# Hybrid decoder layer on one core: the norm row spread into PSUM by a product, z gated once per head, and the late weight and u sums of z's Winograd scheme on VectorE

## Chip, core and metric

The kernel runs on one core of a Trainium2 chip. The metric is device time in microseconds (us) from start to end of the program; the kernel before was run three times on the device: 1046.83, 1048.23 and 1048.41 us, median 1048.23. One more execution was taken with a profile, and all rows below are from that one.

## What is computed

One decoder layer over 16 learned meta tokens and 1024 tokens of width 1024, in fp32:

```python
u = rmsnorm(h, norm_w)                       # h: 1040 x 1024
proj = u @ w_in                              # 1024 x 7184, split into
q, k, v, g_attn, c_b, c_c, c_h, g_conv, z, xbc, dt = split(proj)
y_attn = diff_attention(q, k, v) * silu(g_attn)      # 4 heads
y_conv = short_conv(c_b, c_c, c_h) * silu(g_conv)
y_ssm  = group_norm(ssd_scan(xbc, dt) * silu(z))     # 16 heads in 4 groups
h = h + concat(y_attn, y_conv, y_ssm) @ w_out
out = rmsnorm(h, final_norm_w)[16:]
```

## The kernel before, in words

All products run on TensorE as three fp32r products of high and low parts (high x high, high x low, low x high). A matrix is split by a copy into fp32r (high) and a subtraction (low).

Every engine runs its own queue in the order of hand-written lists of steps: `ahead()` and `BETWEEN` (the x stage), `Z_ACT`, `Z_DVE` and `z_run` of each engine (the z stage), `BEHIND` (its name in the program is `PRE`: the first q, k, v pieces and the dt row), then `schedule()`, once for each of four heads (attention, short convolution, state scan), and at last the output product. Semaphores hold a step until what it reads is there.

**The x stage** (`ahead`, lines 195 to 222). Nine tiles of x (tile 0 is the 16 meta tokens) are loaded, squared and summed on ScalarE (`x_square`), raised to -1/2 on GpSimd (`x_power`, L1047 `power`), scaled on VectorE by that factor and the norm row (`x_scale`, L1462), turned on TensorE (`x_turn`, L1870) into PSUM banks 2 and 3, and split into `u_hi` (`x_high`, ScalarE, L1251) and `u_lo` (`x_low`, VectorE, L1468). The norm row is loaded by a DMA that repeats it over 128 partitions of `lot` (`norm_load`, L890). For tiles 5 to 8, `s1` (L1473) keeps the sum of the two halves of u.

**z** (1024 tokens x 1024 columns) is made by Winograd's scheme: seven products of half the size, in this order: M_11, M_12, M_S2, M_S1, M_S3, M_S4, M_22. Each has four slots (a slot is a quarter of the inner dimension: 4 token tiles x 3 matmuls of 512 columns, L1904). The slots of M_11 and M_12 (0 to 7) are `z_early`, woven between the turns of the x stage, three tile-slots per x tile; slots 8 to 27 are `z_run` on TensorE. Weights come in four blocks T1 to T4 of 1 MB (`z_weights`, each as two DMAs of 512 KB); `z_sum` makes T1-T3, T2-T1, T2-T3 and T4-T2 in place on GpSimd (L1072), after which T2 is loaded a second time for M_S4. The sums of u are `s2` (from `s1`; tiles 0 and 1 on GpSimd, L1077, 2 and 3 on VectorE, L1478) and `s3` (8 steps of two instructions, GpSimd, L1089 and L1090). Weight slots are split by `z_high` (ScalarE, L1196) and `z_low` (L1064 on GpSimd up to slot 7, L1497 on VectorE from slot 8). `z_acc` (ScalarE, L1224) copies a bank out of PSUM, `z_add` (VectorE, L1504) adds a second one to it. Each finished 128 x 512 block is gated here: `z_tanh` (ScalarE, L1235), `z_gate` (VectorE, L1508), 16 of each; then it is stored (`z_store`) to a DRAM scratch, from which each head loads its 128 x 8 x 256 slice (`z_load`, at the end of its attention).

**The state scan of a head** (`schedule`, from `add("chunk", 0)`, line 343). `chunk` c turns and scales the inputs of chunk c (TensorE, then VectorE L1732 to L1739) and multiplies the decay matrix by C.B (L1743, what TensorE's `scan` c needs); `decay` c makes that matrix (ScalarE, L1349 and L1352) from a row that a DMA brings. The end of `scan` on VectorE multiplies by z (L1762). Between the steps, `fill` puts projection pieces (L1885, 3 matmuls for each of 8 slices of the inner dimension) on TensorE. The order on VectorE is chunk 0, chunk 1, scan 0, chunk 2, scan 1, and so on; on ScalarE, decay 1, decay 2.

Of the kernel before, what the change touches and what calls it, by code (L numbers as in the profile page):

```python
# [194 lines left out]
def ahead():  # L195

    out = [("x_load", 0), ("x_load", 1), ("norm_load", 0), ("x_load", 2), ("z_weights", ("T3", 0)), ("x_load", 3),
# [4 lines left out]
    for r in range(-3, CH):  # L202
# [34 lines left out]
def schedule(last):  # L237
# [114 lines left out]
    for c in range(1, CH + 3):  # L352
# [52 lines left out]
Z_ACT = [*[("z_acc", (0, t)) for t in range(4)], ("s2_high", 0), ("s2_high", 1), ("z_high", 8), ("z_high", 9), ("s2_high", 2), ("s2_high", 3), ("z_tanh", (0, 0)), ("z_tanh", (0, 1)),  # L405
         ("z_high", 10), ("z_high", 11), ("z_tanh", (0, 2)), ("z_tanh", (0, 3)), *[("s1_high", t) for t in range(4)], ("z_high", 12),
# [44 lines left out]
def build(nc, x, meta_tokens, norm_w, w_in, w_out, attn_lambda, attn_norm_w, sconv_w, ssm_conv_w,  # L451
# [6 lines left out]
    with ExitStack() as ctx:  # L458
# [105 lines left out]
        norm_row = lot[:, 0:D]  # L564
# [12 lines left out]
        z_th = [lot[:, HALF * n:HALF * (n + 1)] for n in range(2)]  # L577
        s_f = z_th
# [89 lines left out]
        u_ps = [ps[:, 2, :], ps[:, 3, :]]  # L668

# [168 lines left out]
        def _(eng):  # L838
# [187 lines left out]
        def _(eng):  # L1026
# [22 lines left out]
            def z_run():  # L1049
                iteration(-1, [("s2", 0, 1), ("s2", 1, 1), ("z_sum", ("T2", 1), 1), ("z_sum", ("T3", 0), 1), ("z_sum", ("T3", 1), 1),  # L1050
                               *[("s3", (M_S3, k), 1) for k in range(ZK)], ("z_sum", ("T4", 0), 1), ("z_sum", ("T4", 1), 1),
                               *[("s3", (M_S4, k), 1) for k in range(ZK)]])

            def iteration(i, steps):
                for step, a, d in steps:
# [9 lines left out]
                    elif step == "z_sum":  # L1065
                        name, half = a
                        x, y, done = {"T1": ("T1", "T3", 0), "T2": ("T2", "T1", 1 + half), "T3": ("T2", "T3", 3 + half), "T4": ("T4", "T2", 3 + half)}[name]
                        if name in ("T1", "T2"):
                            eng.wait_ge(z_in[name], 32)
# [3 lines left out]
                    elif step == "s2" and a < 2:  # L1073
# [4 lines left out]
                        eng.tensor_tensor(to, to, u_lo[:, 0:ZK, cols].bitcast(F32), ALU.subtract).then_inc(s2p_ok, 1)  # L1078
                    elif step == "s3":

                        p, k = a
                        cols = slice(META + HALF, L) if p == M_S3 else slice(META, META + HALF)
                        q = (M_S3, M_S4).index(p) * ZK + k
                        if q == 0:
                            eng.wait_ge(z_out_ok, 4)
# [1101 lines left out]
```

## Time and profile before

| | |
|---|---|
| runs | 1046.83, 1048.23, 1048.41 us |
| profiled execution | 1048.38 us |
| its span, first to last instruction | 1046.7 us |
| TensorE busy | 1002.3 us (96%) |
| VectorE, ScalarE, GpSimd busy | 693.0, 465.1, 315.1 us |
| x and z stage | from 0 to 119.75 us |
| heads, and the output product | the rest |

Times in rows are microseconds from the start of the span; PE is TensorE, DVE VectorE, ACT ScalarE, POOL GpSimd, SP the queue that issues the DMAs. L1904 is line 1904 of the kernel. A row of a timeline gives start and duration; in brackets stands how long the engine was idle before it, and what ended that.

### The profile page before, as it was taken

The page shows a single profiled execution, that of the slowest core. Times are in us where ns is not written, and L with a number is a line of the kernel's source. Part 1 is how long each engine was busy: PE and PEld are TensorE (multiplying, and loading weights), DVE is VectorE, ACT ScalarE, POOL GpSimd, SP SyncE. Part 2 cuts the span into 40 slices and gives each one's busy share as a digit, 9 for nine tenths or more (in the row PEclk, how much of TensorE's full clock was granted, in tenths as well). Part 3 has the DMA queues.
Part 4 walks back from the last instruction along what each step waited for, and adds up shares of the span by engine and source line. Part 5 has one row for each costly group of instructions (what it writes and reads, how often), then busy time and mean ns, then how long its engine had stood idle before and what let it go on. Part 6 is the DMA issues. An engine that isn't in the chain of part 4 may idle for free.

```text
span 1046.7 us, 15633 instructions
## 1 busy us (share of the span) xinstructions
PE 1002.3 (96%) x5745; PEld 895.0 (86%) x5745; DVE 693.0 (66%) x1238; ACT 465.1 (44%) x1057; POOL 315.1 (30%) x250
## 2 busy tenths in 40 slices
PE   5879999999999999999999999999999979999997
PEld 4657879998989999899899988989998877888885
DVE  5899553777566268656526865663686757698866
ACT  6554333342445443344634433454343454534555
POOL 5956210333333233323321423332151431000002
PEclk9999999999999999999999999999999999999999
DMA  8013402033412303332140333122233330994323
GB/s 343 1 41 103 144 21 84 25 118 101 120 52 71 121 21 121 101 111 61 54 133 26 121 101 111 54 59 92 71 121 100 92 111 2 361 394 146 94 59 161
DMA packets 106807, 110.61 MB, mean 106 GB/s; under 512 B 6374, under 2 KB 76108, under 8 KB 106732
## 3 DMA queue, kind: packets, MB, share of 16 engines
q1 hardware_dynamic: 106732, 109.62, 32.2%
q8 instruction: 46, 0.75, 0.3%
q14 instruction: 29, 0.24, 0.1%
HBM read 84.36 MB, written 25.24 MB: 105 GB/s over the span
## 4 chain that ended last, share of the span: by engine, by line
PE 81%; DVE 6%; issue 5%; POOL 4%; ACT 2%; DMA 1%; SPq 0%; DVEq 0%; ACTq 0%; POOLq 0%
PE ps L1885 45%; PE ps L1894 15%; PE ps L1870 4%; PE ps L2096 3%; PE ps L1904 2%; PE ps L2130 2%; PE ps L2074 2%; PE ps L2075 2%; POOL w_lo L1059 1%; PE ps L2132 1%; PE ps L2136 1%; DVE work L1462 1%; DMA acum_b<-in_w_in 1%; POOL lot L1090 1%; POOL lot L1089 1%
## 5 line engine op out<-in xcount | busy, mean ns | idle before, releaser
L1885 PE MATMUL ps<-u_hi,w_hi 128*128 128x348 f32 (+3 forms) x1024 | 365.2, 357 | 1.8 <-POOL w_lo L1059 1.8
L1885 PE MATMUL ps<-u_lo,w_hi 128*128 128x348 f32 (+3 forms) x1024 | 347.8, 340 | 0.0
L1885 PE MATMUL ps<-u_hi,w_lo 128*128 128x348 f32 (+3 forms) x1024 | 347.2, 339 | 0.0
L1885 PEld LDWEIGHTS ps<-u_hi,w_hi 128*128 128x128 f32 x1024 | 193.5, 189 | 15.0 <-POOL w_lo L1059 2.1
L1059 POOL TENSOR_TENSOR w_lo<-w_raw,w_hi 128x1024 fp32r<-128x1024 f32 x48 | 117.5, 2450 | 293.3 <-ACT w_hi L1183 293.3
L1885 PEld LDWEIGHTS ps<-u_hi,w_lo 128*128 128x128 f32 x1024 | 192.9, 188 | 11.0
L1885 PEld LDWEIGHTS ps<-u_lo,w_hi 128*128 128x128 f32 x1024 | 193.3, 189 | 10.4
L1047 POOL TENSOR_TENSOR small<-small,m_half 128x1 f32<-128x1 f32 (+2 forms) x57 | 46.0, 809 | 311.4 <-DVE small L1824 143.9
L1667 DVE TENSOR_REDUCE small<-ps 128x1 f32<-128x144 f32 (+7 forms) x64 | 49.6, 774 | 82.2 <-PE ps L2078 81.6
L1331 ACT ACTIVATE work<-ps,small 128x144 f32<-128x144 f32 (+7 forms) x64 | 48.1, 751 | 53.8 <-DVE small L1667 53.8
L1870 PE MATMUL ps<-ident,work 128*128 128x128 f32 (+2 forms) x393 | 59.2, 281 | 8.0 <-DVE u_lo L1468 4.4
L1359 ACT ACTIVATE y_n<-y_n,small 128x256 f32<-128x256 f32 x32 | 16.3, 509 | 111.4 <-POOL small L1047 111.4
L1743 DVE TENSOR_TENSOR lm_buf<-lm_buf,lot 128x512 f32<-128x512 f32 x32 | 25.1, 784 | 58.2 <-PE ps L2136 41.6
L1894 PE MATMUL ps<-q_hl 128*128 128x512 f32 x264 | 62.1, 389 | 0.0
L1870 PEld LDWEIGHTS ps<-ident,work 128*128 128x128 f32 (+2 forms) x393 | 45.9, 139 | 14.9 <-issue 9.4
L1894 PEld LDWEIGHTS ps<-q_hl 128*128 128x128 f32 x264 | 49.5, 188 | 10.3
L1349 ACT ACTIVATE lm_buf<-acum_b,sg 128x128 f32<-128x128 f32 x128 | 40.8, 389 | 22.2 <-DMA acum_b<-acum_scratch 16.1
L1183 ACT CAST w_hi<-w_raw 128x1024 fp32r<-128x1024 f32 x48 | 49.8, 1040 | 0.1
L2096 PE MATMUL ps<-conv_b_s,conv_g 128*128 128x128 f32 x288 | 39.3, 282 | 0.0
L1104 POOL TENSOR_TENSOR xdd<-xdt,sg 128x256 f32<-128x256 f32 (+1 forms) x32 | 20.5, 645 | 62.3 <-DVE xdt L1732 62.3
L2074 PE MATMUL ps<-k_hl,q_hl 128*128 128x512 f32 (+4 forms) x112 | 37.8, 338 | 0.3
L2075 PE MATMUL ps<-k_hl,q_hl 128*128 128x512 f32 (+4 forms) x112 | 36.3, 335 | 0.0
(391 smaller groups left out, 1855.3 us busy)
## 6 DMA issues: line engine op xcount, KB each, us to landing
w_raw<-in_w_in SPq DMA_DIRECT2D x48, 512.0 KB, 4.4
acum_b<-acum_scratch SPq DMA_DIRECT2D x32, 256.0 KB, 4.4
acum_b<-in_w_out SPq DMA_DIRECT2D x22, 256.0 KB, 4.6
work<-in_x SPq DMA_DIRECT2D x8, 512.0 KB, 9.4
work<-in_w_out SPq DMA_DIRECT2D x16, 256.0 KB, 4.1
t_scratch<-work SPq DMA_DIRECT2D x16, 256.0 KB, 2.3
t_scratch<-acum_b SPq DMA_DIRECT2D x16, 256.0 KB, 2.6
work<-z_scratch SPq DMA_DIRECT2D x4, 1024.0 KB, 5.3
```

The costliest lines, as they stand in the source:

```text
L1047: return eng.tensor_tensor(to[0:rows_, n:n + w], of[0:rows_, n:n + w], m_half[0:rows_, 0:w], ALU.pow)
L1059: eng.tensor_tensor(w_lo[:, a % 2, :, :], w_raw[:, a % 2, :, :], w_hi[:, a % 2, :, :].bitcast(F32), ALU.subtract).then_inc(w_lo_ok, 1)
L1183: eng.copy(w_hi[:, b, :, :], w_raw[:, b, :, :]).then_inc(w_hi_ok, 1)
L1331: eng.activation(prob[m][:, 0:nk], s_ps[:, 0:nk], ACT.Exp, bias=mx[:, m:m + 1], accum_out=psum_e[:, s % 2, m:m + 1]).then_inc(exp_ok, 1)
L1349: ins = eng.activation(lmat[:, a % 2, r, :], acum_b[:, a % 2, r, :], ACT.Relu, bias=sg[:, 1, a, r:r + 1], scale=-1.0)
L1667: eng.tensor_reduce(mx[:, m:m + 1], s_ps[:, 0:nk], AX.X, ALU.max, negate=True).then_inc(max_ok, 1)
L1870: return eng.transpose(dst, src, ident[0:n, 0:n])
L1885: ins = eng.matmul(dst, w[:, k, 0:m], u[:, k, cols], start=(k == 0 and n == 0), stop=(k == KD - 1 and n == 2))
L1894: ins = eng.matmul(ps[:, BANKS[n // KS][t], :], y[:, at], w, start=(begins and m == 0), stop=(ends and m == 2), skip_group_check=True)
L2074: eng.matmul(s_ps[:, at:end], q_hi[m][:, qs], k_st[m][:, at:end], start=True, stop=False)
L2075: ins = eng.matmul(s_ps[:, at:end], q_lo[m][:, qs], k_st[m][:, at:end], start=False, stop=not masked)
L2096: eng.matmul(o_ps[:, P:2 * P], a_t[:, n, :], v_blk[:, n, :], start=(n == 0), stop=False)
```

## The change

- The norm row is loaded once (4 KB, first in SP's queue) and spread over 128 partitions by two fp32 products with a row of ones into PSUM banks 5 and 6 (`norm_row`); `x_scale` reads it there. M_12's first two tiles, which use these banks, now wait for the last `x_scale`.
- In the x stage GpSimd does the sums for T1 two rounds earlier (rounds 2 and 3), T2's first in round 5, T2's second in round 7, and all four `s2`.
- `s3` and the sums for T3 and T4 move from GpSimd's `z_run` into `Z_DVE`, each two or three steps ahead of its use.
- z is stored without the gate (z's third block by `z_acc` (2, t) instead of tanh and gate out of PSUM). Each head gates its slice in two halves of 128 x 1024: `z_tanh` 0 and `z_gate` 0 after `decay` 1 and in front of chunk 1; `z_tanh` 1 and `z_gate` 1 behind chunk 2. They use `th_tile`.
- `w_dt`'s DMA counts on the semaphore of the other parameter rows.

```diff
 def ahead():
-    out = [("x_load", 0), ("x_load", 1), ("norm_load", 0), ("x_load", 2), ("z_weights", ("T3", 0)), ("x_load", 3),
+    out = [("norm_load", 0), ("norm_row", 0), ("x_load", 0), ("x_load", 1), ("x_load", 2), ("z_weights", ("T3", 0)), ("x_load", 3),
...
         if r >= 5:
             out.append(("s1", r - 5))
+            if r == 7:
+                out.append(("z_sum", ("T2", 1)))
+            if r >= 6:
+                out.append(("s2", r - 6))
...
 BETWEEN = [...
-           ("z_high", 4, 2), ("z_low", 4, 2), ("z_high", 5, 3), ("z_low", 5, 3), ("z_high", 6, 4), ("z_low", 6, 4), ("z_high", 7, 5), ("z_low", 7, 5),
-           ("z_sum", ("T1", 0), 5), ("z_sum", ("T1", 1), 6), ("z_sum", ("T2", 0), 7)]
+           ("z_high", 4, 2), ("z_low", 4, 2), ("z_sum", ("T1", 0), 2), ("z_sum", ("T1", 1), 3), ("z_high", 5, 4), ("z_high", 6, 4), ("z_low", 5, 4), ("z_low", 6, 4),
+           ("z_high", 7, 5), ("z_low", 7, 5), ("z_sum", ("T2", 0), 5)]
...
     add("chunk", 0)
     add("decay", 1)
+    add("z_tanh", 0)
+    add("z_gate", 0)
...
         if c < CH:
             add("chunk", c)
+        if c == 2:
+            add("z_tanh", 1)
+            add("z_gate", 1)
...
+Z_ACT = [("s2_high", 0), ("s2_high", 1), ("z_high", 8), ("s2_high", 2), ("z_acc", (0, 0)), ("z_acc", (0, 1)), ("s2_high", 3), ("z_acc", (0, 2)), ("z_acc", (0, 3)),
+         *[("z_high", n) for n in (9, 10, 11)], *[("s1_high", t) for t in range(4)], ("z_high", 12),
...
-         *[("z_tanh", (1, t)) for t in range(4)], *[("z_high", n) for n in range(23, 28)], *[("z_tanh", (2, t)) for t in range(4)]]
+         *[("z_high", n) for n in range(23, 28)], *[("z_acc", (2, t)) for t in range(4)]]
...
+Z_DVE = [("s2_low", 0), ("s2_low", 1), ("z_low", 8), ("s2_low", 2), ("s2_low", 3), ("z_low", 9), ("z_low", 10), ("z_low", 11), *[("z_add", (0, t)) for t in range(4)],
+         *[("s1_low", t) for t in range(4)], ("z_low", 12), ("s3", (M_S3, 0)), ("s3", (M_S3, 1)), ("z_low", 13), ("s3_low", (M_S3, 0)), ("s3", (M_S3, 2)), ("z_sum", ("T3", 0)),
+         ("z_low", 14), ("s3_low", (M_S3, 1)), ("s3", (M_S3, 3)), ("z_sum", ("T3", 1)), ("z_low", 15), ("z_low", 16), ("s3_low", (M_S3, 2)), ("s3", (M_S4, 0)),
+         ("z_low", 17), ("s3_low", (M_S3, 3)), ("s3", (M_S4, 1)), ("z_low", 18), ("s3_low", (M_S4, 0)), ("s3", (M_S4, 2)), ("z_sum", ("T4", 0)),
+         ("z_low", 19), ("s3_low", (M_S4, 1)), ("s3", (M_S4, 3)), ("z_sum", ("T4", 1)), ("s3_low", (M_S4, 2)), ("z_low", 20), ("s3_low", (M_S4, 3)), ("z_low", 21),
+         ("z_low", 22), *[("z_add", (1, t)) for t in range(4)], *[("z_low", n) for n in range(23, 28)]]
...
-        norm_row = lot[:, 0:D]
+        norm_row = lot[0:1, 0:D]
...
-        z_th = [lot[:, HALF * n:HALF * (n + 1)] for n in range(2)]
+        z_th = th_tile[:, 0:D].rearrange("p (c n) -> p c n", c=QB // 2)
...
+        norm_ps = ps[:, 5:7, :].rearrange("p b n -> p (b n)")
...
-                        eng.dma_start(norm_row, norm_w[0, :].partition_broadcast(P)).then_inc(norm_in, 16)
+                        eng.dma_start(norm_row, norm_w[0:1, :]).then_inc(norm_in, 16)
...
             def z_run():
-                iteration(-1, [("s2", 0, 1), ("s2", 1, 1), ("z_sum", ("T2", 1), 1), ("z_sum", ("T3", 0), 1), ("z_sum", ("T3", 1), 1),
-                               *[("s3", (M_S3, k), 1) for k in range(ZK)], ("z_sum", ("T4", 0), 1), ("z_sum", ("T4", 1), 1),
-                               *[("s3", (M_S4, k), 1) for k in range(ZK)]])
+                iteration(-1, [("s2", 3, 1)])
...
                     elif step == "z_tanh":
...
+                        eng.wait_ge(z_n_in, 16 * (it + 2))
+                        if a == 0:
+                            eng.wait_ge(conv_ok, it * 4 + 5)
                         else:
...
+                            eng.wait_ge(z_out_ok, it * 2 + 1)
+                        eng.activation(z_th, z_n[:, 4 * a:4 * a + 4, :], ACT.Tanh, scale=0.5).then_inc(z_th_ok, 1)
...
                     elif step == "z_gate":
...
+                        half = slice(4 * a, 4 * a + 4)
+                        eng.wait_ge(z_th_ok, it * 2 + a + 1)
+                        eng.scalar_tensor_tensor(z_n[:, half, :], z_th, 1.0, z_n[:, half, :], ALU.add, ALU.mult).then_inc(z_out_ok, 1)
...
-                            eng.wait_ge(z_n_in, 16 * (it + 2))
+                            eng.wait_ge(z_out_ok, it * 2 + (a - 1) // 4 + 1)
...
+                    elif step == "norm_row":
+                        eng.wait_ge(norm_in, 16)
+                        for h in range(2):
+                            ins = eng.matmul(norm_ps[:, HALF * h:HALF * (h + 1)], ones[0:1, :], norm_row[:, HALF * h:HALF * (h + 1)], start=True, stop=True)
+                        ins.then_inc(norm_pe, 1)
...
+                            if ZY_BANKS[t] in (5, 6) and p == M_12:
+                                eng.wait_ge(x_n, CH)
```

SP's wait for `z_sum_ok` 8 (all eight sums) in front of T2's second load stands in both versions.

## Rows read from the trace of the kernel before

**Rows 1.** Waits of TensorE, whole span: total, times, longest.
```profile
PE ps L1904 <- DVE w_lo L1497: 9.2, 5, 3.9
```

**Rows 2.** Timeline of PE: restarts in the x and z stage, and the first projection.
```profile
39.76 0.89 PE L1870 MATMUL ps<-ident,work 128*128 128x128 f32 x4 [1.84 <-DVE xd L1473]
...
56.05 0.50 PE L1904 MATMUL ps<-w_hi,k_hl 128*128 128x512 f32 x1 [3.89 <-DVE w_lo L1497]
...
97.66 0.50 PE L1904 MATMUL ps<-w_hi,q_hl 128*128 128x512 f32 x1 [0.34 <-DVE w_lo L1497]
...
119.75 0.32 PE L1885 MATMUL ps<-u_hi,w_hi 128*128 128x348 f32 x1
```

**Rows 3.** Windows: busy us (instructions) of PE, PEld, DVE, ACT, POOL; PEclk, DMA share, GB/s.
```profile
10.00:20.00 10.00, 6.15 (x23) 5.24 (x24) 6.52 (x12) 6.66 (x13) 7.20 (x7) 1.00 1.04 415
...
56.00:60.00 4.00, 3.95 (x11) 3.18 (x12) 4.00 (x7) 2.23 (x5) 0.00 (x0) 0.63 0.04 8
```

**Rows 4.** Timeline of POOL: a z_low, the last power, a sum alone, an s3 beside DVE.
```profile
29.68 1.27 POOL L1064 TENSOR_TENSOR q_hl<-lm_buf,q_hl 128x512 fp32r<-128x512 f32 x1
...
33.85 0.55 POOL L1047 TENSOR_TENSOR small<-small,m_half 128x1 f32<-128x1 f32 x1
34.37 2.37 POOL L1072 TENSOR_TENSOR conv_b_s<-conv_b_s,acum_b 128x1024 f32<-128x1024 f32 x1
...
66.88 1.74 POOL L1089 TENSOR_TENSOR lot<-u_hi,w_raw 128x512 f32<-128x512 f32 x1
```

**Rows 5.** DMA issues: size, us from issue to landing; and SP's issue of T1's second half.
```profile
lot<-in_norm_w SPq DMA_DIRECT2D x1, 512.0 KB, 5.3
...
conv_b_s<-in_w_in SPq DMA_DIRECT2D x1, 512.0 KB, 13.3
...
th_tile<-in_w_in SPq DMA_DIRECT2D x1, 512.0 KB, 4.9
...
10.33 0.49 SPq L897 DMA_DIRECT2D conv_b_s<-in_w_in  x1
```

**Rows 6.** Timeline of DVE: x_scale 8, x_low 7, one s2 instruction, four z_add, a 128x1024 two-operand product.
```profile
34.54 3.28 DVE L1462 SCALAR_TENSOR_TENSOR work<-work,small,lot 128x1024 f32<-128x1024 f32 x1
37.74 1.28 DVE L1468 TENSOR_TENSOR u_lo<-ps,u_hi 128x512 fp32r<-128x512 f32 x2
...
53.98 0.68 DVE L1478 TENSOR_TENSOR w_raw<-y_n,u_hi 128x512 f32<-128x512 f32 x1
...
99.55 2.48 DVE L1504 TENSOR_TENSOR ys<-ps,ys 128x512 f32<-128x512 f32 x4
...
881.20 1.22 DVE L1718 TENSOR_TENSOR conv_y<-conv_y,conv_b_s 128x1024 f32<-128x1024 f32 x1
```

**Rows 7.** Timeline of ACT: last instruction of decay 1 in the first, third and last head.
```profile
267.80 0.63 ACT L1352 ACTIVATE lm_buf<-lm_buf 128x512 f32<-128x512 f32 x1
...
641.07 0.64 ACT L1352 ACTIVATE lm_buf<-lm_buf 128x512 f32<-128x512 f32 x1
...
826.71 0.63 ACT L1352 ACTIVATE lm_buf<-lm_buf 128x512 f32<-128x512 f32 x1
```

**Rows 8.** Chain of waits, pieces in order of time (start, us): scan 1 on PE, same heads.
```profile
271.99 0.84 PE ps L2130 x8
...
644.39 0.84 PE ps L2130 x8
...
828.70 0.84 PE ps L2130 x8
```

**Rows 9.** Timelines of ACT and DVE, first head: a tanh, a gating product, chunk 1's first and last steps.
```profile
260.77 1.08 ACT L1316 ACTIVATE th_tile<-work 128x1040 f32<-128x1040 f32 x1 [2.93 <-DVE work L1645]
...
261.88 1.24 DVE L1654 SCALAR_TENSOR_TENSOR work<-th_tile,work 128x1040 f32<-128x1040 f32 x1 [0.48 <-ACT th_tile L1316]
...
264.26 0.42 DVE L1732 TENSOR_TENSOR xdt<-ps,sg 128x256 f32<-128x256 f32 x1
...
268.46 0.69 DVE L1743 TENSOR_TENSOR lm_buf<-lm_buf,lot 128x512 f32<-128x512 f32 x1 [2.93 <-ACT lm_buf L1352]
```

More of the change, by code:

```diff
@@ L576, in build @@
         s2_f = w_raw_flat.rearrange("p (k n) -> p k n", k=ZK)
-        z_th = [lot[:, HALF * n:HALF * (n + 1)] for n in range(2)]
-        s_f = z_th
+        z_th = th_tile[:, 0:D].rearrange("p (c n) -> p c n", c=QB // 2)
+        s_f = [lot[:, HALF * n:HALF * (n + 1)] for n in range(2)]
         z_tmp = [[work[:, D * 4 + HALF * t:D * 4 + HALF * (t + 1)] for t in range(4)],
@@ L1072, in iteration @@
                         eng.tensor_tensor(z_w[name][half], z_w[x][half], z_w[y][half], ALU.subtract).then_inc(z_sum_ok, 1)
-                    elif step == "s2" and a < 2:
+                    elif step == "s2":
                         cols = slice(META + P * a, META + P * (a + 1))
@@ L1077, in iteration @@
                         own(eng, eng.tensor_tensor(to, s1_f[a].rearrange("p (k n) -> p k n", k=ZK), u_hi[:, 0:ZK, cols].bitcast(F32), ALU.subtract))
[L1078 to L1085, printed above, removed]
[L1086 to L1090 removed]
+                        eng.tensor_tensor(to, to, u_lo[:, 0:ZK, cols].bitcast(F32), ALU.subtract).then_inc(s2_ok, 1)
                     elif step == "x_power":
@@ L1473, in iteration @@
                         eng.tensor_tensor(s1_f[a], u_ps[1], s1_f[a], ALU.add).then_inc(s1_ok, 1)
-                    elif step == "s2" and a >= 2:
-                        cols = slice(META + P * a, META + P * (a + 1))
-                        to = s2_f[:, :, P * a:P * (a + 1)]
-                        eng.wait_ge(s1_ok, a + 1)
-                        own(eng, eng.tensor_tensor(to, s1_f[a].rearrange("p (k n) -> p k n", k=ZK), u_hi[:, 0:ZK, cols].bitcast(F32), ALU.subtract))
-                        eng.tensor_tensor(to, to, u_lo[:, 0:ZK, cols].bitcast(F32), ALU.subtract).then_inc(s2d_ok, 1)
+                    elif step == "s3":
+                        p, k = a
+                        cols = slice(META + HALF, L) if p == M_S3 else slice(META, META + HALF)
+                        q = (M_S3, M_S4).index(p) * ZK + k
+                        if q == 0:
+                            eng.wait_ge(norm_pe, 1)
+                            eng.wait_ge(s2_ok, 4)
+                        if q >= 2:
+                            eng.wait_ge(s_lo_ok[M_S3 if q - 2 < ZK else M_S4], (q - 2) % ZK + 1)
+                        own(eng, eng.tensor_tensor(s_f[q % 2], u_hi[:, ZK + k, cols].bitcast(F32), s2_f[:, k, :], ALU.subtract))
+                        eng.tensor_tensor(s_f[q % 2], s_f[q % 2], u_lo[:, ZK + k, cols].bitcast(F32), ALU.add).then_inc(s3_ok, 1)
+                    elif step == "z_sum" and a[0] in ("T3", "T4"):
+                        name, half = a
+                        x, y = {"T3": ("T2", "T3"), "T4": ("T4", "T2")}[name]
+                        eng.wait_ge(z_sum_ok, 3 + half)
+                        eng.tensor_tensor(z_w[name][half], z_w[x][half], z_w[y][half], ALU.subtract).then_inc(z_sum_ok, 1)
                     elif step == "s2_low":
```

69 lines of the change are left out of this document (23 added, 46 removed).

## Prediction, made before the result

> **What bounds the kernel now.** I read the page's busy shares first: TensorE works 96% of the span, so a change can win only in a stretch where it waits. The view of its waits places most of them: 9.2 us for `z_low` on VectorE (L1497) [rows 1], all in the z stage. The timeline of TensorE shows where: idle 1.84 us before tile 8's turn at 39.76, 3.89 us before M_S2 at 56.05, a short wait before M_S4 at 97.66; M_22 ends and the projections begin at 119.75 [rows 2]. From 97.66 on it runs through: 96 matmuls in 22.09 us, 0.230 us each. After the long wait the granted clock averaged 0.63 from 56 to 60 [rows 3], so a wait can cost more than its length. Everything behind 119.75 is a row of projections: what ends the z stage earlier moves all of it, and a wait added in a head adds to it. So there are two sums, the front's and the heads'.
>
> **The front: x stage.** GpSimd now does T1's first sum in round 2, and that sum waits for T1's weights. Today the second half is issued at 10.33 and lands 13.3 us later, at 23.6 [rows 5]. The 512 KB norm load ahead of it [rows 5] shrinks to 4 KB; at 415 GB/s [rows 3] that is 1.3 us, so 22.3. From there GpSimd's queue is the clock of the x stage, since `x_power` of tiles 5 to 8 stands behind the sums: to the end of power 8, three sums of 2.37, three `z_low` of 1.27 and four powers of 0.55 [rows 4], 13.1 us, make 35.4, against 34.4 now (33.85 + 0.55) [rows 4]. A later power, but `x_scale` 8 took 3.28 us with both operands in SBUF while GpSimd summed; the `x_low` pair behind it reads one operand from PSUM and took 1.28 for two, also beside a GpSimd sum [rows 6]. I take 1.3 for `x_scale` from PSUM (bounds 1.3 and 3.3), as that is the nearer kind. It ends at 36.8 instead of 37.8; two `x_low` and an `s1`, 1.9 us, then tile 8's turn at 38.8 instead of 39.76. The two M_12 tile-slots that now wait for `x_scale` 8 fit before it. Behind it TensorE has 14 tile-slots x 3 x 0.230 and two sets of turns of about 0.4: 10.4 us, M_12's end at 49.2, against 52.2 now (56.05 - 3.89) [rows 2].
>
> Norm product: no row shows it; between nothing and several us. It delays the first `x_scale`s, which run ahead of T1's landing, and that cover I count as holding: nothing. If it is gone, tiles 5 to 8 slip by as much. The norm load now stands first in SP's queue, so each x load issues about 0.5 us later [rows 5]; same cover.
>
> **The front: z stage.** After power 8, GpSimd does `s2` 0, T2's second sum, and `s2` 1 to 3: eight instructions of 1.27 and one of 2.37, 12.5 us, to 47.9, if nothing disturbs it; 1.74 each where VectorE interleaves two-operand steps [rows 4], up to 1.9 for four of them: 49.8. I take 49.5, because `Z_DVE` begins at about 42.5. The Trainium skill, SBUF — State Buffer, section "Who interferes with whom", has the shared port pair as an exclusive lock held for the whole instruction, the loser blocked; by that rule four whole VectorE steps of 0.62 would stand in GpSimd's way, `s2` 3 would end about 0.6 us later and so would the sum. Behind `s2` 3, ScalarE has `s2_high` 3, two `z_acc` and `z_high` 9, about 2.3 us: VectorE takes `z_low` 9 at 51.8.
>
> From there VectorE has no wait in my walk, and no competitor, as GpSimd's queue is empty: to T4's second sum it has 25 single steps of 0.62 (four took 2.48), eight `s3` of two instructions of 0.68, four sums of 1.22 [rows 6]: 15.5 + 10.9 + 4.9 = 31.3 us, so 83.1. Then SP, which waits for all eight sums, reloads T2: the second issue about 0.5 us behind, 4.9 to landing [rows 5]: 88.5; `z_high` 20 and `z_low` 20, 1.2 us: M_S4 starts at 89.7 instead of 97.66. TensorE itself could be there sooner: M_S2 from 49.2, with M_S1 and M_S3 48 matmuls each, 33.1 us, and about 3 us waiting for `z_acc` (3, 0), which ScalarE reaches only behind `s3_high`: 85.3. So **T2's reload is late next**, and it covers whatever the clock costs before. M_S4 and M_22 are the same 22.1 us; the projections begin at 111.8, 8.0 us earlier. The wait before M_S4 is some 4 us; one of 3.89 us was followed by four at 0.63 [rows 2, 3], 1.5 us lost. I take half: the **front gains 7.2**, bounds 4 and 9.
>
> The weight splits of the first pieces need M_S4's last bank, `z_acc` (2, t), two casts and two GpSimd subtractions: some 9 us beside M_22's 11. The removed 16 tanh and 16 gates lay on ScalarE and VectorE beside products; M_S4's path is in the walk, the others were covered. `w_dt`'s shared semaphore: nothing, as SP issues that load and the rows in one go, in front of the first projection weights. SP's stores wait for less than before.
>
> **The heads.** `z_gate` 0 stands on VectorE between chunk 0 and chunk 1, and waits for `z_tanh` 0, which ScalarE reaches only after decay 1. Queued behind it is all of chunk 1, with L1743, for which TensorE's scan 1 waits. In the first head decay 1 ends at 268.43 [rows 7] and scan 1 starts at 271.99 [rows 8]: 3.56 us. Now to go between: tanh 1.08, gate 1.24, chunk 1's small steps 1.27 (264.26 to 265.53, that is 268.46 - 2.93), L1743 0.69 [rows 9], together 4.28. TensorE waits 0.7. The second head repeats it (0.7 taken). In the third decay ends at 641.71 and scan 1 starts at 644.39: 2.68, so 1.6. In the last, which has half the fill between the scans, 827.34 and 828.70: 1.36, so 2.9 [rows 7, 8]. The sum is 5.9; bounds 4 (if the decay row lands sooner) and 8 (if the lower clock follows the long wait in the last head). The second half's tanh and gate (2.3 us) fall in VectorE's wait for scan 1 on TensorE: 0.1. **The heads lose 6.0.** Projections follow without slack, so these add up.
>
> **Sum.** The profiled execution took 1048.38, 1.7 over its span, and 0.15 over the median. 1048.4 - 7.2 + 6.0 = **1047.2**, 1.0 under the median. A measurement can tell about 0.2% (2.1 us) from no change.
>
> **Rivals.**
> - *The gate hides.* If decay 1 starts about 1.5 us sooner in every head, or TensorE arrives later, the heads cost about 1, and the front's gain stands: 1042. For it: decay waits for a DMA, and its end varies by 0.9 us against scan 1 between the first and third head [rows 7, 8]. Against: no edit moves that DMA. Chance 0.2.
> - *The VectorE list is slower than its steps.* One mechanism: `Z_DVE` now holds `s3` and the sums, and every step that has to wait for ScalarE pushes T4's last sum and so T2's reload. If M_S4 starts after 93.6 (front gain under 4.1), the heads outweigh it by over 2.1 us; at 95.5 the gain is 2.2 and the time 1052. For it: three engines pass `s3`, high and low round; against: in the walk ScalarE is ready each time. Chance 0.2.
> - *PSUM doesn't free `x_scale`* (the change doesn't do that part): 2.0 us more on `x_scale` 8, 1049; part of the forecast's range.
>
> **How the numbers follow.** Forecast 0.6, centred on 1047.2, 1044.5 to 1049.5 by itself; a third of it lies under 1046.1 (0.2% faster), the rest within 0.2%. With the rivals: faster 0.2 + 0.2 = 0.4; same 0.4; slower 0.2. The range for 8 in 10 takes in the first rival's centre and stops just short of the second's: 1042 to 1051.5.
>
> **What would show it.** Right: POOL's T1 sum in the low twenties with power 5 behind it; `x_scale` at 1.3; T4's last sum near 83 on DVE, T2's issue behind it, M_S4 near 90; the first L1885 near 112; and in each head a TensorE wait at L2130 for L1743, longest in the last. Wrong: no such wait in the heads, or M_S4 starting at the end of M_S3 without one, or after 93.6.

## The result, and the profile after

The change made the kernel slower: 1051.81 us, the median of 8 runs, against 1048.37 for 8 runs of the kernel before on the same chip, ratio 1.0023, 95% interval 1.0012 to 1.0033. Forecast was 1047.2, range 1042 to 1051.5. The profiled execution took 1051.7, its span 1049.9, 3.2 more than before.

First the waits of TensorE in the changed kernel (total, times, longest):

```profile
PE ps L1876 <- ACT y_n L1354: 7.4, 6, 4.0
PE ps L2143 <- DVE lm_buf L1749: 5.1, 4, 2.7
PE ps L1910 <- DVE w_lo L1503: 4.0, 1, 4.0
PE ps L1891 <- POOL w_lo L1069: 1.8, 1, 1.8
```

The first line stands for `y_n`, a chunk's output after gate and norm, which TensorE turns at the end of its scan; it was 7.0 in six before. The 9.2 us for `z_low` [rows 1] have become one wait of 4.0, and the waits for L1749 (L1743 of the kernel before, and of the prediction) are new: 5.1 in four. Where they lie, from TensorE's timeline of the changed kernel; the lines answer to [rows 2] and [rows 8]:

```profile
39.92 0.63 PE L1876 MATMUL ps<-ident,work 128*128 128x128 f32 x4 [0.69 <-DVE xd L1468]
63.24 0.47 PE L1910 MATMUL ps<-w_hi,s_work 128*128 128x512 f32 x1 [1.41 <-ACT xdt L1220]
89.77 0.51 PE L1910 MATMUL ps<-w_hi,q_hl 128*128 128x512 f32 x1 [4.02 <-DVE w_lo L1503]
113.47 0.32 PE L1891 MATMUL ps<-u_hi,w_hi 128*128 128x348 f32 x1
147.03 0.42 PE L1891 MATMUL ps<-u_hi,w_hi 128*128 128x348 f32 x1 [1.81 <-POOL w_lo L1069]
267.96 1.08 PE L2143 MATMUL ps<-xdt,lm_buf 128*128 128x64 f32 x8 [0.74 <-DVE lm_buf L1749]
455.34 1.08 PE L2143 MATMUL ps<-xdt,lm_buf 128*128 128x64 f32 x8 [0.93 <-DVE lm_buf L1749]
642.49 1.08 PE L2143 MATMUL ps<-xdt,lm_buf 128*128 128x64 f32 x8 [0.74 <-DVE lm_buf L1749]
829.80 1.07 PE L2143 MATMUL ps<-xdt,lm_buf 128*128 128x64 f32 x8 [2.73 <-DVE lm_buf L1749]
864.80 0.44 PE L1876 MATMUL ps<-ident,y_n 128*128 128x128 f32 x2 [3.99 <-ACT y_n L1354]
```

And three places of the kernel before that [rows 2] doesn't have: the third weight tile of the first projections, scan 0 of the last head, and the turn of its fourth y_n:

```profile
153.39 0.43 PE L1885 MATMUL ps<-u_hi,w_hi 128*128 128x348 f32 x1 [1.80 <-POOL w_lo L1059]
823.50 0.67 PE L2136 MATMUL ps<-xdd,lot 16*128 16x256 f32 x2 [0.68 <-POOL xdd L1104]
861.46 0.44 PE L1870 MATMUL ps<-ident,y_n 128*128 128x128 f32 x2 [3.60 <-ACT y_n L1359]
```

M_S4 starts at 89.77 and the projections at 113.47, 6.28 earlier than before [rows 2]. So front and heads went as walked, and yet the kernel lost. The same places in both timelines show where:

| TensorE starts | before | after | after minus before |
|---|---|---|---|
| third weight tile (waits 1.8 for `w_lo` in both) | 153.39 | 147.03 | -6.36 |
| scan 0, first head | 264.90 | 260.13 | -4.77 |
| scan 0, second head | 451.10 | 447.32 | -3.78 |
| scan 0, third head | 637.30 | 634.66 | -2.64 |
| scan 0, last head | 823.50 | 821.88 | -1.62 |
| scan 1, last head | 828.54 | 829.80 | +1.26 |
| turn of the first y_n, last head | 838.64 | 841.57 | +2.93 |
| turn of the fourth y_n | 861.46 | 864.80 | +3.34 |
| span | 1046.7 | 1049.9 | +3.2 |

A head's scan 1 comes 0.99, 1.14, 1.02 and 2.88 later than before: the wait, and 0.15 to 0.3 more that no wait shows. But two steps of the table have no new wait in them: 1.59 between 147 and 260, and 1.67 between scan 1 and the first y_n of the last head. The stretches behind three of the waits, with columns as in [rows 3], the granted clock (PEclk) behind POOL, show what they are. The changed kernel:

```profile
90.00:94.00 4.00, 4.00 (x12) 3.09 (x12) 4.00 (x8) 3.15 (x7) 0.00 (x0) 0.57 1.09 274
148.00:152.00 4.00, 4.00 (x18) 4.00 (x17) 1.07 (x4) 0.00 (x0) 1.67 (x1) 0.57 0.47 131
831.00:834.00 3.00, 3.00 (x11) 2.73 (x10) 1.59 (x3) 1.40 (x5) 3.00 (x2) 0.50 0.02 5
```

And the kernel before, behind the same 1.80 us wait and behind its scan 1 in the last head:

```profile
153.00:157.00 4.00, 3.61 (x23) 3.61 (x24) 1.48 (x5) 0.59 (x1) 2.72 (x2) 1.00 0.47 131
829.00:832.00 3.00, 3.00 (x20) 2.90 (x20) 1.99 (x4) 2.87 (x8) 1.91 (x2) 1.00 0.38 111
```

Clock 0.57 over four microseconds is 1.7 us lost; 0.50 is the lower of the two levels, 1.2 GHz. In the changed kernel TensorE went to it behind M_S4's wait (where the kernel before paid about as much behind M_S2's, [rows 3]), behind the unchanged wait of 1.8, and behind the last head's 2.73. (Both kernels have one more such stretch, behind the wait for the fourth y_n.) The account of the profiled pair is: front -6.36, heads +6.03, two more stretches at half clock +1.59 and +1.67, the fourth y_n +0.41, the rest -0.1: +3.2.

The front, row by row (VectorE, GpSimd, ScalarE and SP's queue of the changed kernel), beside [rows 4, 5, 6]:

```profile
22.57 2.00 POOL L1081 TENSOR_TENSOR conv_g<-conv_g,conv_u 128x1024 f32<-128x1024 f32 x1 [0.88 <-DMA conv_b_s<-in_w_in]
34.81 0.55 POOL L1059 TENSOR_TENSOR small<-small,m_half 128x1 f32<-128x1 f32 x1
35.84 1.27 DVE L1457 SCALAR_TENSOR_TENSOR work<-work,small,ps 128x1024 f32<-128x1024 f32 x1
47.69 1.62 POOL L1087 TENSOR_TENSOR w_raw<-w_raw,u_lo 128x512 f32<-128x512 f32 x1
51.49 0.69 DVE L1503 TENSOR_TENSOR w_lo<-conv_y,w_hi 128x512 fp32r<-128x512 f32 x1 [0.80 <-ACT w_hi L1193]
81.30 1.22 DVE L1485 TENSOR_TENSOR lm_buf<-lm_buf,th_tile 128x1024 f32<-128x1024 f32 x1
82.97 0.94 SPq L906 DMA_DIRECT2D th_tile<-in_w_in  x1
88.37 0.62 ACT L1193 CAST w_hi<-conv_y 128x512 fp32r<-128x512 f32 x1 [9.79 <-DMA th_tile<-in_w_in]
```

T1's sum, which the change moves from rounds 5 and 6 to 2 and 3 (three rounds earlier, not two), starts at 22.57 (walked: 22.3), power 8 ends at 35.36 (35.4), `x_scale` 8 at 37.1 (36.8), the last `s2` at 49.3 (49.5), `z_low` 9 starts at 51.5 (51.8), T4's last sum ends at 82.5 (83.1), M_S4 starts at 89.77 (89.7).

The last head (ScalarE, VectorE):

```profile
825.57 1.04 ACT L1228 ACTIVATE th_tile<-work 128x1024 f32<-128x1024 f32 x1
826.64 1.23 DVE L1514 SCALAR_TENSOR_TENSOR work<-th_tile,work 128x1024 f32<-128x1024 f32 x1 [5.34 <-ACT th_tile L1228]
828.97 0.68 DVE L1749 TENSOR_TENSOR lm_buf<-lm_buf,lot 128x512 f32<-128x512 f32 x1
```

VectorE stands 5.34 us idle in front of the gate with chunk 1 queued behind it; L1749 ends at 829.65, and TensorE begins scan 1 at 829.80.

### The profile page after: what moved, and what is told of

It reads as the page before. It is cut to its first block, busy times and chain, and to the rows that moved or that the text cites. A ratio compares the mean times of both kernels' runs of the same rounds, so it can differ in the third digit from the quotient of the medians.

```text
span 1049.9 us, 15623 instructions
## 1 busy us (share of the span) xinstructions
PE 1008.2 (96%) x5749; PEld 899.5 (86%) x5749; DVE 680.2 (65%) x1246; ACT 465.5 (44%) x1053; POOL 281.5 (27%) x234
## 4 chain that ended last, share of the span: by engine, by line
PE 78%; DVE 7%; POOL 4%; DMA 4%; issue 3%; ACT 2%; SPq 1%; DVEq 0%; ACTq 0%; POOLq 0%
PE ps L1891 43%; PE ps L1900 15%; PE ps L1876 3%; PE ps L2109 3%; PE ps L2143 2%; DMA acum_b<-acum_scratch 2%; PE ps L1910 2%; PE ps L2087 2%; PE ps L2088 2%; POOL small L1059 1%; PE ps L2145 1%; DMA conv_b_s<-in_w_in 1%; PE ps L2149 1%; DVE work L1651 1%; DVE small L1706 1%
## 5 line engine op out<-in xcount | busy, mean ns | idle before, releaser
L1673 DVE TENSOR_REDUCE small<-ps 128x1 f32<-128x144 f32 (+7 forms) x64 | 49.5, 774 | 82.2 <-PE ps L2091 81.7
L1749 DVE TENSOR_TENSOR lm_buf<-lm_buf,lot 128x512 f32<-128x512 f32 x32 | 25.3, 789 | 39.0 <-PE ps L2149 34.6
L2143 PEld LDWEIGHTS ps<-xdt,lm_buf 128*128 128x128 f32 x256 | 32.4, 192 | 6.8 <-issue 6.2
L2087 PE MATMUL ps<-k_hl,q_hl 128*128 128x512 f32 (+4 forms) x112 | 37.9, 338 | 0.2
```

The costliest lines, as they stand in the source:

```text
L1673: eng.tensor_reduce(mx[:, m:m + 1], s_ps[:, 0:nk], AX.X, ALU.max, negate=True).then_inc(max_ok, 1)
L2087: eng.matmul(s_ps[:, at:end], q_hi[m][:, qs], k_st[m][:, at:end], start=True, stop=False)
L2143: eng.matmul(y_ps[b][:, r * HD:(r + 1) * HD], lmat[:, b, r, :], xdt[:, b, r * HD:(r + 1) * HD], start=True, stop=True)
```

## The experiments

The question: are the missing 3.3 us the price of TensorE's idle time in clock, and can both waits (the gate's, T2's) be taken away? Rival: the half-clock stretches have nothing to do with the waits. Medians, ratios to runs of the kernel before on the same chip, and the granted clock averaged over all runs of each:

| run | median us | ratio, 95% interval | mean clock |
|---|---|---|---|
| change, as given | 1051.81 | 1.0023 (1.0012 to 1.0033) | 0.9909 |
| change, again, with e6 to e8 | 1052.95 | 1.0036 (1.0025 to 1.0048) | 0.9904 |
| before, with e5 to e8 | 1048.94 | 1 | 0.9926 |
| e1 gate behind chunk 1 | 1047.08 | 0.9969 (0.9956 to 0.9983) | 0.9920 |
| e2 T4's sums early | 1045.92 | 0.9966 (0.9954 to 0.9978) | 0.9931 |
| e3 useless matmuls in the change | 1050.21 | 1.0005 (0.9995 to 1.0015) | 0.9931 |
| e4 gating alone | 1054.81 | 1.0045 (1.0028 to 1.0063) | 0.9906 |
| e6 e1 and e2 together | 1041.33 | 0.9924 (0.9911 to 0.9936) | 0.9940 |
| e7 and a weight split earlier | 1041.61 | 0.9929 (0.9914 to 0.9945) | 0.9938 |
| e8 norm row back in SBUF | 1060.12 | 1.0108 (1.0090 to 1.0126) | 0.9878 |
| e9 useless matmuls in before | 1049.10 | 1.0005 (0.9993 to 1.0016) | 0.9940 |
| e10 e6 with useless matmuls | 1040.53 | 0.9923 (0.9907 to 0.9939) | 0.9963 |

**e1, the gate behind chunk 1.**

```diff
     add("decay", 1)
     add("z_tanh", 0)
-    add("z_gate", 0)
...
         if c < CH:
             add("chunk", c)
+        if c == 1:
+            add("z_gate", 0)
```

> The changed kernel with one step moved: in every head the first half's gate stands on VectorE behind chunk 1 instead of ahead of it. Theory (each head's wait is the gate queued ahead of L1749, and the long wait of the last head also costs a stretch at half clock behind it, 831.9 to 834.0, about 1.6 us): TensorE's four waits for L1749 go (scan 1 came 0.9, 1.1, 0.9 and 2.9 later than it would have, 5.8 together), the half-clock stretch in the last head goes too: 1051.8 - 5.8 - 1.6 = 1044.4. Rival 1 (the gate is only moved: 1.24 us on VectorE then delay the copies and sums behind scan 1, or chunk 2's L1749, and TensorE waits there): 1048 to 1051. Rival 2 (the half-clock stretch has nothing to do with that wait): 1046.0, with a stretch at half clock still near the last head's scan 1.

Measured: 0.9969, which is 5.7 us under the change's first ratio (1.0023) and 7.0 under its second (1.0036). No wait for L1750 (the change's L1749) is left in any head; a head takes 186.25 again, as before, instead of 187.2 to 187.3. VectorE of the last head, where chunk 1's product now comes first and the gate behind it:

```profile
823.31 0.69 DVE L1750 TENSOR_TENSOR lm_buf<-lm_buf,lot 128x512 f32<-128x512 f32 x1 [3.17 <-ACT lm_buf L1348]
824.26 1.23 DVE L1515 SCALAR_TENSOR_TENSOR work<-th_tile,work 128x1024 f32<-128x1024 f32 x1 [0.26 <-ACT th_tile L1229]
```

What the theory missed is, against the first ratio, some 1.7 us: in the last head TensorE now waits 1.87 for the first y_n (0.21 in the change). On VectorE both gates stand ahead of that y_n in either kernel, but in e1 the step between them, chunk 2's product, begins while GpSimd subtracts a weight tile (827.07 to 829.48) and takes 2.92; first e1, then the change:

```profile
827.11 2.92 DVE L1750 TENSOR_TENSOR lm_buf<-lm_buf,lot 128x512 f32<-128x512 f32 x1
```

```profile
832.58 0.96 DVE L1749 TENSOR_TENSOR lm_buf<-lm_buf,lot 128x512 f32<-128x512 f32 x1 [1.41 <-PE ps L2149]
```

So rival 1 holds for a small part, in the last head only. The half clock near 831 went with the wait.

**e2, T4's sums early.**

```diff
-         ("z_low", 17), ("s3_low", (M_S3, 3)), ("s3", (M_S4, 1)), ("z_low", 18), ("s3_low", (M_S4, 0)), ("s3", (M_S4, 2)), ("z_sum", ("T4", 0)),
-         ("z_low", 19), ("s3_low", (M_S4, 1)), ("s3", (M_S4, 3)), ("z_sum", ("T4", 1)), ("s3_low", (M_S4, 2)), ("z_low", 20), ("s3_low", (M_S4, 3)), ("z_low", 21),
+         ("z_low", 17), ("s3_low", (M_S3, 3)), ("z_sum", ("T4", 0)), ("z_sum", ("T4", 1)), ("s3", (M_S4, 1)), ("z_low", 18), ("s3_low", (M_S4, 0)), ("s3", (M_S4, 2)),
+         ("z_low", 19), ("s3_low", (M_S4, 1)), ("s3", (M_S4, 3)), ("s3_low", (M_S4, 2)), ("z_low", 20), ("s3_low", (M_S4, 3)), ("z_low", 21),
```

> The changed kernel with T4's two sums moved forward on VectorE, from behind s3 2 and s3 3 of M_S4 to just behind the last low round of M_S3's sums. Theory (M_S4 waits for T2's second load, which waits for the last sum; a 4.02 us wait, and behind it 90 to 94 at 0.57 of the clock, 1.7 us): the last sum ends near 76 instead of 82.5, T2 lands near 82, M_S4 starts at M_S3's end, 85.8, and the half-clock stretch at 90 goes: 1051.8 - 4.0 - 1.7 = 1046.1. Rival 1 (the sums, 2.4 us, delay z_low 18 and 19, for which M_S3 has 4.5 and 3.6 us of slack, and TensorE waits inside M_S3): 1048 to 1050. Rival 2 (the wait goes, but the clock falls at the next wait instead): 1047.8, with as many half-clock stretches as before.

Measured: 0.9966, 6.0 us under the change's first ratio and 7.3 under its second. The chain to M_S4 on VectorE, SP and ScalarE, and TensorE at the third weight tile:

```profile
74.15 1.22 DVE L1485 TENSOR_TENSOR lm_buf<-lm_buf,th_tile 128x1024 f32<-128x1024 f32 x1
75.82 0.47 SPq L906 DMA_DIRECT2D th_tile<-in_w_in  x1
80.69 0.62 ACT L1193 CAST w_hi<-conv_y 128x512 fp32r<-128x512 f32 x1 [0.36 <-DMA th_tile<-in_w_in]
140.70 0.43 PE L1891 MATMUL ps<-u_hi,w_hi 128*128 128x348 f32 x1 [1.80 <-POOL w_lo L1069]
```

M_S4 has no wait, no stretch under full clock lies between 62 and 140, and the third weight tile starts 6.33 earlier than in the change: 4.02 of wait, about 1.7 of clock, and 0.4 that it was ahead at M_S1 already (62.86 for 63.24). The theory holds; the rivals don't.

**e3, useless matmuls in the wait of the last head.**

```diff
                             eng.wait_ge(y_gated, it * QB + max(a - 2, 0) + 1)
+                            if steps is LAST and a == 1:
+                                for _ in range(5):
+                                    eng.matmul(y_ps[b][:, 0:GW], c_t[:, ca:cb], xs[:, 0, 0:GW], start=True, stop=True)
                             eng.wait_ge(g_ok, it * QB + a + 1)
```

> The changed kernel with five matmuls (128 columns by 256, some 0.44 us each, 2.2 us together) added on TensorE in the last head, between the fill and the wait for L1749 ahead of scan 1; they write the part of the bank that scan 1 overwrites, so the result is the same. Theory (the wait lowers the clock): TensorE's wait falls from 2.73 to about 0.5, scan 1 starts when it did (829.8), and the stretch at half clock behind it (831.9 to 834.0) goes: useless work makes the kernel 1.6 us faster, 1050.2. Rival (the half-clock stretch is not caused by the idle time): the same time, 1051.8, and the stretch is still there.

Measured: 1.0005 against 1.0023 and 1.0036 for the change: 1.9 to 3.3 us less. The stretch behind scan 1, first with the useless matmuls, then in the change without them:

```profile
832.00:835.00 3.00, 3.00 (x23) 2.98 (x23) 2.96 (x5) 0.61 (x1) 1.49 (x2) 1.00 0.30 87
```

```profile
832.00:835.00 3.00, 3.00 (x14) 2.91 (x13) 2.42 (x2) 1.91 (x5) 2.01 (x2) 0.60 0.01 2
```

The wait in front of L1749 is 0.51, the clock stays, and the three microseconds have 23 matmuls in them instead of 14. From scan 1 to the first y_n it takes 10.67 instead of 11.77: 1.1, as 0.45 (0.66 for 0.21) of the gain goes into a longer wait for that y_n. The theory holds: with the idle time filled and nothing else changed, the clock did not fall there.

**e4, the gating alone**, in the kernel before: the hunks of the change on `z_tanh`, `z_gate`, `z_store` and `z_acc` (2, t), nothing else.

```diff
-         *[(name, (3, t)) for name in ("z_add", "z_tanh", "z_gate") for t in range(4)], ("w_dt", 0),
+         *[("z_add", (3, t)) for t in range(4)], ("w_dt", 0),
...
     add("decay", 1)
+    add("z_tanh", 0)
+    add("z_gate", 0)
...
```

> The kernel before with one part of the change alone: z stored ungated, tanh and gate per head (two halves, placed as in the change); norm row, sums and their engines as before. Theory: the heads cost what they cost in the change, 5.8 us of waits and 1.6 at half clock in the last head, 0.4 in the last norms, and the 16 tanh and 16 gates that leave the z stage free nothing there: 1048.4 + 7.8 = 1056.2. Rival 1 (the gates that leave the front's queues let VectorE reach z_low and the sums sooner, and the front gains 2 to 4): 1052 to 1054. Rival 2 (the heads' loss came from the front's shift in time, not from the gate): within 1 us of 1048.4.

Measured: 1.0045, 4.9 us over the kernel before, between theory and rival 1, and rival 1's mechanism is there: the front gains 3.1. TensorE at the third weight tile (before: 153.39) and at the last head's scan 1:

```profile
150.29 0.43 PE L1891 MATMUL ps<-u_hi,w_hi 128*128 128x348 f32 x1 [1.80 <-POOL w_lo L1067]
833.21 1.30 PE L2136 MATMUL ps<-xdt,lm_buf 128*128 128x64 f32 x8 [2.72 <-DVE lm_buf L1749]
```

So taking the gate out of the z stage gains 3.1 in the old front, where the whole change gains 6.4; whether it is worth as much within the change is not shown. The heads cost what they cost in the change: a scan 1 later by 0.8 to 1.3 three times, and by 2.9.

**e5, the change again**, unaltered.

> The changed kernel unaltered, for a second profile and beside the others on one chip. Theory (waits are fixed, half-clock stretches behind them are drawn anew in each run, the likelier the longer the wait): the same waits within 0.3 us (1.8 for w_lo in the first projections, some 0.9 three times and 2.7 for L1749), half clock again behind the waits of over 2 us (M_S4, the last head's scan 1, the fourth y_n), and perhaps not behind the 1.8; ratio to before 1.0023 as at first. Rival (the stretches belong to the kernel's places, not to the waits): the same four stretches, the one near 148 too.

Measured: 1.0036; over all its runs the clock is 0.9904 against 0.9926 for the kernel before, on one chip. One minus the clock, times the time, is 10.1 against 7.7 us: by this count some 2.3 of the 3.7 between the two means is clock. The waits came again as 3.52 for M_S4, 1.80, and 0.78, 0.92, 1.25 and 2.80 for L1749, with half clock behind 3.52, 2.80, the fourth y_n and, again, the 1.80. This run by itself tells nothing against the rival; the other profiles do (below).

**e6, both moves**, e1 and e2 together.

> The gate behind chunk 1 and T4's sums early, together. Theory (the two losses lie in different stretches and add): from the ratios to before of the changed kernel (1.0023), the gate moved (0.9969) and the sums moved (0.9966), 0.9912 of before, 1040.7 where before takes 1049.9; no TensorE wait of over 1.9 us between M_S1 and the norms of the last head. Rival (an overlap: what one frees the other finds already free, or a new wait turns up in the last head): 0.994 to 0.996.

Measured: 0.9924, 7.6 us faster than the kernel before and 11.6 faster than the change beside it. The losses lie in different stretches and add. Scan 0 of the first and of the second head on TensorE, 186.21 apart and 12.4 sooner than before:

```profile
252.46 0.67 PE L2150 MATMUL ps<-xdd,lot 16*128 16x256 f32 x2 [0.68 <-POOL xdd L1102]
438.67 0.67 PE L2150 MATMUL ps<-xdd,lot 16*128 16x256 f32 x2 [0.68 <-POOL xdd L1102]
```

**e7, the third weight tile split earlier as well.**

```diff
-          ("parameters", 0), ("lambda", 0), ("lambda_end", 0), *piece(TQ, 1)[:1], ("dt_end", 0), *piece(TQ, 1)[1:], ("split", 2), ("load", 3),
+          ("parameters", 0), ("lambda", 0), ("lambda_end", 0), *piece(TQ, 1)[:1], ("dt_end", 0), piece(TQ, 1)[1], ("split", 2), piece(TQ, 1)[2], ("load", 3),
```

> As the run with both moves, and ScalarE casts the third weight tile (split 2) one step earlier, ahead of its work on the last q piece, so that GpSimd's subtraction, for which TensorE waits 1.8 us in the first projections, starts about 2.4 us sooner. Theory: TensorE then waits for the q piece's bank instead, about 1.1 us (1.05 of cast ahead of VectorE's last step, which ended just as the projection could begin), 0.7 less, and too short a wait for the clock to fall behind it, which half of the profiles had (1.6): 0.7 to 2.3 us under the run with both moves. Rival (the q piece's delay costs as much as the cast gains): the same as both moves.

Measured: 0.9929, the same as e6. A miss: the wait changed its releaser and grew from 1.80 to 2.43.

```profile
142.11 0.40 PE L1892 MATMUL ps<-u_hi,w_hi 128*128 128x348 f32 x1 [2.43 <-DVE q_hl L1620]
```

**e8, the norm row back in SBUF**, in the change.

```diff
-    out = [("norm_load", 0), ("norm_row", 0), ("x_load", 0), ("x_load", 1), ("x_load", 2), ("z_weights", ("T3", 0)), ("x_load", 3),
+    out = [("x_load", 0), ("x_load", 1), ("norm_load", 0), ("x_load", 2), ("z_weights", ("T3", 0)), ("x_load", 3),
...
-                        eng.dma_start(norm_row, norm_w[0:1, :]).then_inc(norm_in, 16)
+                        eng.dma_start(norm_row, norm_w[0, :].partition_broadcast(P)).then_inc(norm_in, 16)
...
-                        eng.scalar_tensor_tensor(x_buf[a][0:n, 0:D], x_buf[a][0:n, 0:D], rs[0:n, a:a + 1], norm_ps[0:n, :], ALU.mult, ALU.mult).then_inc(x_n, 1)
+                        eng.scalar_tensor_tensor(x_buf[a][0:n, 0:D], x_buf[a][0:n, 0:D], rs[0:n, a:a + 1], norm_row[0:n, :], ALU.mult, ALU.mult).then_inc(x_n, 1)
...
```

> The changed kernel with the norm row undone: the 512 KB broadcast load into SBUF, in its old place in SP's queue, no norm product on TensorE, x_scale with both operands in SBUF. Theory: T1 lands 1.3 us later, x_scale 8 takes about 3.3 instead of 1.27 while GpSimd sums, tile 8's turn comes about 3 us later than 39.9, and the z stage behind it, whose VectorE list runs without a gap to T4's last sum, shifts by as much: 3 us slower than the changed kernel (1.0052 of before). Rival (M_S4's wait or the x stage's slack hides it): within 0.5 us of the changed kernel.

Measured: 1.0108, 7.2 us over the change beside it, more than twice what was expected. VectorE's `x_scale` and GpSimd beside it:

```profile
26.30 3.37 DVE L1457 SCALAR_TENSOR_TENSOR work<-work,small,lot 128x1024 f32<-128x1024 f32 x1 [2.32 <-POOL small L1059]
30.85 1.83 DVE L1457 SCALAR_TENSOR_TENSOR work<-work,small,lot 128x1024 f32<-128x1024 f32 x1
31.56 2.25 POOL L1074 TENSOR_TENSOR q_hl<-lm_buf,q_hl 128x512 fp32r<-128x512 f32 x1
35.45 1.72 DVE L1457 SCALAR_TENSOR_TENSOR work<-work,small,lot 128x1024 f32<-128x1024 f32 x1
36.04 3.37 POOL L1081 TENSOR_TENSOR conv_y<-conv_y,conv_g 128x1024 f32<-128x1024 f32 x1
```

It hits both engines: a sum that began 0.59 behind an `x_scale` takes 3.37 instead of 2.39, a `z_low` 2.25 instead of 1.29. I had priced one late `x_scale`; four of them (3.37, 1.83, 1.72 and 2.30) slow the sums in GpSimd's queue too, and M_S1 starts at 69.17 instead of 63.24. The sum at 36.04 ended 2.24 after the `x_scale` did (35.45 + 1.72 = 37.17; 36.04 + 3.37 = 39.41), about its usual length: it stood still until then. That is what the Trainium skill, SBUF — State Buffer, section "Who interferes with whom", says of an engine that comes second. With the row in PSUM no `x_scale` takes over 1.28 and no sum over 2.39. By the two profiles 5.7 of the loss is there at scan 0 of the first head; the rest comes in the heads and in the clock. e8 also has the 512 KB load back (T1's sum starts at 23.75) and keeps the change's order of sums on GpSimd, so 7.2 is the price of all that in the changed kernel, not in the kernel before.

**e9 and e10, useless matmuls ahead of the fourth y_n**, in the kernel before and in e6.

```diff
+                        eng.wait_ge(ys_ok, it * QB + a)
+                        if steps is LAST and a == 4:
+                            for _ in range(8):
+                                eng.matmul(yt_ps[:, 0:2 * P], tri[:, :], xs[:, 0, 0:2 * P], start=True, stop=True)
                         eng.wait_ge(y_n_ok, it * QB + a)
-                        eng.wait_ge(ys_ok, it * QB + a)
```

> The kernel before with nothing of the change, but eight matmuls without a use (128 columns by 256, some 0.44 us each, 3.5 us together) on TensorE in the last head, just ahead of its longest wait there, 3.60 us for the fourth y_n, behind which 862.5 to 864.4 ran at half clock; they write the bank that the transposes behind the wait overwrite. Theory (the idle time lowers the clock): the wait falls to about 0.2, the transposes start when they did (861.5), the half clock behind them does not come, and the kernel is 1 to 1.6 us faster than before, 0.9987 of it. Rival (the half clock belongs to that place or that time, not to the idle TensorE): 1.000, with the stretch still there.

> Both moves, and the same eight matmuls ahead of the wait for the fourth y_n (4.19 us, behind it 852.5 to 856 at half clock). Theory: the wait falls to about 0.7, the stretch at half clock goes, 1.6 us under the run with both moves: 0.991 of before. Rival: the same as both moves, 0.9924.

Measured: 1.0005 and 0.9923, no gain in either, though the clock did what the theory says. The filler and the stretch behind it in e9 (clock there 0.60 in the kernel before):

```profile
859.09 3.72 PE L2147 MATMUL ps<-work,tri 128*128 128x256 f32 x16 [1.37 <-ACT ys L1366]
```

```profile
862.00:865.00 3.00, 3.00 (x21) 2.86 (x20) 0.10 (x1) 2.16 (x8) 0.00 (x0) 1.00 0.04 13
```

(The trace has two records for each of the eight matmuls.) The filler had to wait 1.37 for ScalarE to read the bank that it writes, so it ended at 862.8 and held the turns up by about 1.3 us, what the clock gave back. The mean clock rose (to 0.9940 in e9 from 0.9926 in the kernel before on that chip, to 0.9963 in e10 from 0.9940 in e6), the time did not fall.

**Which waits the clock follows.** Over all twelve profiles, every wait of TensorE of 1.2 us or more between 45 and 900 us, and whether the granted clock went to half in it or within 4 us behind it:

| TensorE idle, us | waits | followed by half clock |
|---|---|---|
| 1.20 to 1.58 | 35 | 0 |
| 1.80 to 1.91 | 15 | 6 |
| 2.08 to 3.09 | 15 | 10 |
| 3.10 to 5.23 | 16 | 16 |

The 1.80 us wait for `w_lo` is in eleven of them, the same to 0.01 us, and the clock fell behind it in five. And no stretch at half clock between 45 and 900 us lies anywhere but in or behind one of these waits. So the half clock belongs to idle time and not to a place, which ends the rival. The length of a wait alone doesn't settle it: of five waits of 2.40 to 2.43 two were followed by half clock. What decides for waits of middle length, and why the 3.09 of the kernel before had none behind it, stays open.

## Why the prediction was wrong

- **The front: 7.2 predicted, 6.3 measured.** On the path to M_S4 the walk was right to 0.6 us at each point (tile 8's turn, 39.92 for 38.8, was off by 1.1; the wait for `z_acc` (3, 0) was 1.41 for about 3, which M_S4's wait covers), and "T2's reload is late next" was right: 4.02 us of wait. The mis-sized term is "I take half" of the clock loss behind that wait; the whole 1.7 came, and M_22's end with it (113.47 for 111.8). e2 gives it back with the wait.
- **What the front consists of** was less clear than I wrote. "PSUM doesn't free `x_scale`" was priced at 2.0 us; the SBUF row costs 7.2 in the changed kernel (e8), since it slows GpSimd's sums too. And the gates that left the z stage, "the others were covered", are worth 3.1 by themselves in the old front (e4). Whether the sums on VectorE gain anything alone wasn't tried.
- **The heads: 6.0 predicted, 6.03 measured** (0.99, 1.14, 1.02, 2.88; I had 0.7, 0.7, 1.6, 2.9). Mechanism and place were right, and e1 shows the cause: with the gate behind chunk 1 the waits are gone. The sum is right partly by luck. The third head waited less than the rows of one execution let expect (1.25 in the change's second profile). And scan 1's starts, read from the chain [rows 8], are 0.16 later than on TensorE's timeline (828.54 for 828.70 in the last head); with the timeline's the same walk gives 6.6.
- **The step that failed** is the clock in the heads. "8 (if the lower clock follows the long wait in the last head)" stood as an outer bound; it was the likely case, 1.67 us: all five profiles with a wait of 2.6 to 2.9 us there had the half clock behind it. A term was missing altogether: a wait that the change does not touch, 1.8 us for `w_lo`, may cost another 1.6 when the draw is worse: it did in both profiles of the change and not in the kernel before. (How often it does so in runs without a profile isn't known.) Together 3.3, and with the fourth y_n's 0.4, this turns -1.2 (after the 0.9 of the front: -0.3) into +3.2.
- **The rival on the other side**, a slow VectorE list with M_S4 after 93.6, did not happen: M_S4 started at 89.77. The time came near that rival's 1052 for another reason. "The gate hides" didn't happen either.
- What I worked out from the Trainium skill, SBUF — State Buffer, section "Who interferes with whom" (`s2` 3 ending 0.6 later) isn't borne out at that place: the step ended at 49.3, before the 49.5 of the walk, in which 1.74 per step already held the contention of [rows 4]. There VectorE was held up more: three of its steps beside `s2` 2 and 3 took 1.78 where such a step takes 0.69 alone.

## What to carry to other kernels

Ask for every wait that a change adds to a TensorE that is otherwise full not only how long it is but whether the clock follows: here the clock fell behind all 16 waits of 3.1 us and more (some 1.7 us lost, in five of them 2.2 to 3.1), behind 16 of the 30 from 1.8 to 3.1, and behind none of the 35 shorter ones. A step that waits for a late engine goes behind the work that others wait for, not ahead of it (moving one `z_gate` was worth 5.7 to 7.0 us), and the sum that releases a reload goes ahead of sums that are not due yet (6.0 to 7.3 us). Filling a wait with useless matmuls kept the clock all three times; it paid in e3, where the filler began with the wait and ended inside it, and not in e9 and e10, where it began late and held up what came behind.

## What the runs showed of the hardware

- The scatter between runs of one kernel is for the most part clock: of 14 runs of the kernel before on one chip, the one with a mean clock of 0.995 took 1047.36 us, those at 0.990 to 0.991 took 1050.83 and 1051.22. In the profile of the change a stretch at half clock is some 3.4 us long (148.3 to 151.7, 831.0 to 834.4) and costs 1.7; runs without a profile show only the mean clock, but by this a run has one stretch more or less rather than a little of everything. Two kernels of one profile each can then differ by 3 us, two such stretches, for this alone (an estimate).
- GpSimd and VectorE hold each other up in both directions when an `x_scale` reads two operands in SBUF: 3.37 instead of 1.27 on VectorE, 3.37 instead of 2.39 on GpSimd (e8).
- A 1 x 1024 row spread over 128 partitions by a product with ones took 3.75 us at the start of the kernel for four passes; it moved the first `x_scale` by 2.7 us (9.76 for 7.06), and T1's sum still began at 22.57, so nothing on the path was late for it.
